# A one-core decode-and-prefill block on Trainium2: state chunks loaded early, masked B made up front, stores issued by ScalarE, first prompt tile turned inside the state stage

## The reference, cut to what matters

```python
proj = h @ w_in                       # z (2048 columns), xbc (3072), dt (32)
xbc = silu(causal_conv(xbc)); xs, Bm, Cm = split(xbc)
dt = softplus(dt + dt_bias); A = -exp(a_log)
# per head of 64 channels, chunks of 128 tokens, state of 64 x 128 per head:
A_cs   = cumsum(A * dt)
y_diag = (C . B) * exp(segsum) @ (xs * dt)
state' = state * exp(A_cs[last]) + B^T . (exp(A_cs[last] - A_cs) * xs * dt)
y_off  = exp(A_cs) * (C . state)
y = (y_diag + y_off + d_skip * xs) * silu(z), then group norm, @ w_out
```

## Time and profile before

| | before |
|---|---|
| median of 3 runs | 2064.46 us (2064.24 to 2065.48) |
| the profiled execution | 2061.77 us |
| its span, first to last instruction | 2060.1 us |
| PE busy | 1868.6 us, 91% |
| DVE busy | 1473.5 us, 72% |
| ACT busy | 1246.7 us, 61% |
| POOL busy | 177.9 us, 9% |
| mean granted clock of TensorE | 0.949 of full |

### The profile page before, as it was taken

One profiled execution on the slowest core, in us unless ns is written; L12 is line 12 of the kernel. 1 busy time (PEld: TensorE's weight loads), 2 busy tenths in 40 slices (PEclk: granted clock), 3 DMA queues, 4 the chain that ended last, 5 costly groups with the idle time before them and its releaser, 6 DMA issues.

```text
span 2060.1 us, 31992 instructions
## 1 busy us (share of the span) xinstructions
PE 1868.6 (91%) x10922; PEld 1608.2 (78%) x10922; DVE 1473.5 (72%) x1769; ACT 1246.7 (61%) x1604; POOL 177.9 (9%) x243
## 2 busy tenths in 40 slices
PE   6978889999889768789769999999999999999994
PEld 6968769999789548688558888888888888888883
DVE  7477436664478455753359888898988889888894
ACT  6555325443367124431268787888878787887873
POOL 2001101000124341010110000000000000000001
PEclk9989899999989889899889999999999999999997
DMA  7544667854434471156469999999999999999993
GB/s 276 193 133 159 243 255 283 352 166 141 160 98 155 170 262 59 46 190 236 184 230 386 370 380 372 380 356 374 378 360 380 374 385 354 372 376 357 393 366 144
DMA packets 151105, 558.74 MB, mean 271 GB/s; under 512 B 16496, under 2 KB 16496, under 8 KB 149568
## 3 DMA queue, kind: packets, MB, share of 16 engines
q1 hardware_dynamic: 139248, 508.58, 67.2%
q0 software_dynamic: 7200, 28.56, 3.7%
q10 hardware_dynamic: 4528, 20.05, 2.4%
HBM read 520.61 MB, written 36.52 MB: 270 GB/s over the span
## 4 chain that ended last, share of the span: by engine, by line
PE 77%; issue 8%; DVE 7%; DMA 4%; ACT 4%; POOL 1%; POOLq 0%; SPq 0%; ACTq 0%; DVEq 0%
PE ps L1663 23%; PE ps L1665 23%; PE ps L1664 23%; DMA raw<-in_stream 2%; DVE w_lo L1059 2%; ACT w_hi L670 2%; PE ps L1949 1%; PE ps L2064 1%; POOL rt L2108 1%; PE ps L1762 1%; PE ps L1793 1%; PE ps L1809 1%; PE ps L1694 1%; DMA y_rows<-ye 0%; PE ps L1784 0%
## 5 line engine op out<-in xcount | busy, mean ns | idle before, releaser
L1564 DVE TENSOR_TENSOR w_lo<-raw,w_hi 128x1024 fp32r<-128x1024 f32 x672 | 787.1, 1221 | 50.6 <-ACT w_hi L989 49.0
L989 ACT ACTIVATE w_hi<-raw 128x1024 fp32r<-128x1024 f32 x672 | 704.6, 1060 | 139.7 <-PE ps L1665 119.9
L1059 DVE TENSOR_TENSOR w_lo<-raw,w_hi 128x1024 fp32r<-128x1024 f32 x212 | 264.3, 1258 | 245.2 <-ACT w_hi L670 243.9
L1663 PE MATMUL ps<-w_hi,xe_hi 128*128 128x512 f32 x896 | 358.2, 400 | 4.7 <-DVE w_lo L1564 4.7
L1665 PE MATMUL ps<-w_hi,xe_lo 128*128 128x512 f32 x896 | 354.5, 396 | 0.0
L1664 PE MATMUL ps<-w_lo,xe_hi 128*128 128x512 f32 x896 | 354.0, 395 | 0.0
L670 ACT ACTIVATE w_hi<-raw 128x1024 fp32r<-128x1024 f32 x212 | 220.5, 1051 | 160.2 <-PE ps L1665 97.2
L1663 PE MATMUL ps<-h_hi,w_hi 128*128 128x288 f32 x928 | 286.1, 308 | 18.4 <-DVE h_lo L1085 14.1
L1664 PE MATMUL ps<-h_lo,w_hi 128*128 128x288 f32 x928 | 280.1, 302 | 0.0
L1665 PE MATMUL ps<-h_hi,w_lo 128*128 128x288 f32 x928 | 278.9, 301 | 0.0
L1663 PEld LDWEIGHTS ps<-h_hi,w_hi 128*128 128x128 f32 x928 | 180.1, 194 | 31.4 <-DVE h_lo L1085 16.8
(11 more groups left out here) (395 smaller groups left out, 2553.1 us busy)
## 6 DMA issues: line engine op xcount, KB each, us to landing
raw<-in_experts SPq DMA_DIRECT2D x672, 512.0 KB, 5.5
raw<-in_stream SPq DMA_DIRECT2D x264, 512.0 KB, 4.4
rest<-in_stream SPq DMA_DIRECT2D x28, 512.0 KB, 5.1
x_rows<-zeros ACTq DMA_DIRECT2D x1, 13824.0 KB, 57.7
out_ssd_s<-s_new POOLq DMA_DIRECT2D x16, 512.0 KB, 4.4
xs<-x_rows POOLq DMA_DIRECT2D x9, 512.0 KB, 4.8
y_rows<-ye POOLq DMA_DIRECT2D x9, 512.0 KB, 7.3
out_k<-kmem ACTq DMA_DIRECT2D x2, 1024.0 KB, 6.6
```

Of the source, the lines that this page charges most:

```text
L989: act.activation(w_hi[:, (NSPLIT + p) % HL, :], raw[:, slot, :], ACT.Copy) \
L1059: dve.tensor_tensor(w_lo[:, o % HL, :], landing_place(k), w_hi[:, o % HL, :].bitcast(F32), ALU.subtract).then_inc(lo_done, 1)
L1564: dve.tensor_tensor(w_lo[:, (NSPLIT + p) % HL, :], raw[:, (NRING + p) % RAW, :], w_hi[:, (NSPLIT + p) % HL, :].bitcast(F32), ALU.subtract) \
L1663: pe.matmul(out, l_hi, r_hi, start=start, stop=False)
```

## The change

- `GATES` becomes [4, 1, 1, 2, 2, 2, 1, 1, 2]: y off 0 and 1 come one z tile apart and earlier.
- The state chunks S0a, S0b and S1a leave the ring. They land in `soon`, 12 KB in the upper part of `zs` (the gates' buffer), and SyncE issues them ahead of xbc 10 once f2's last group is full. The ScalarE gates that write over them wait for y off and `sn_dec` of the chunk. `zs` tile 5 and later wait for S1a's users, tile 8 for S0b's, tile 12 for S0a's.
- AHEAD of the groups s state, y off and xt of tile 0 is capped at two past the need; the cap for the first state chunks starts three chunks later, and for later ones goes by the z tile instead of by the s state two before.
- Masked B of all eight sequences is made before the first add (`btm4` has eight places now). VectorE waits for the store of out_ssd_c there, over whose source `btm4` lies.
- GpSimd only makes the decayed states; ScalarE issues the two stores of batch b (`send`) after the z gates of b.
- acs and last are made once, for the samples and both prompt tiles together, last two xbc tiles after acs. All exps of dec and last_dec are made at the beginning of the state stage.
- xt of tile 0 (transposes and VectorE's products) moves to just before y off 7, into a buffer of its own; y off turn moves behind bt and cb of tile 0.

With the new plan AHEAD of s state 0 is z 6, of s state 1 z 7, 2 z 9, 3 z 11, 4 z 13, 5 z 14, 6 z 15; of the ScalarE gates z 4 and z 5 z 9, z 6 and z 7 z 10, z 8 and z 9 z 12, z 10 and z 11 z 13, z 12 z 15, z 13 ssd out's first chunk, z 14 and z 15 its fifth. In the ring, S1b follows xbc 23, S3a waits for S1b's slot, z 11 for S2a's, S5a for S3a's, S6b for S4a's, S7a for S5a's.

The diff, cut to its core:

```diff
-GATES = [4] + [2, 1] * (NB // 2)
+GATES = [4, 1, 1, 2, 2, 2, 1, 1, 2]
 assert sum(GATES) == KI
+
+SOON, SOON_AT = 3, 10
...
-    p += [(("acs", 2), "dve", 0), (("last", 2), "dve", 0), (("ab", 2), "dve", 0)]
-    p += [(("xbc", c), "act", 1) for c in range(SAMPLE_AT + 1, NXBC)]
+    p += [("acs", "dve", 0)]
+    p += [(("xbc", c), "act", 1) for c in range(SAMPLE_AT + 1, SAMPLE_AT + 3)]
+    p += [("last", "dve", 0), (("ab", 2), "dve", 0)]
+    p += [(("xbc", c), "act", 1) for c in range(SAMPLE_AT + 3, NXBC)]
...
     for b in range(NB):
         p += z[sum(GATES[:b + 1]):sum(GATES[:b + 2])]
+        if b == NB - 1:
+            p += [(("xt", 0, i), "dve", 0) for i in range(4)]
         p += [(("y off", b), "dve" if b == NB - 1 else None, 2)]
         p += [(("s state", b, g), "dve", 0) for g in range(GROUPS)]
-    p += [("y off turn", "dve", 0)]
     for t in range(2):
-        p += [(("acs", t), "dve", 0), (("last", t), "dve", 0)]
-        p += [(("xt", t, i), "dve", 0) for i in range(4)]
+        if t:
+            p += [(("xt", t, i), "dve", 0) for i in range(4)]
         p += [(("bt", t), "act", 0), (("cb", t), "dve", 0)]
+        if t == 0:
+            p += [("y off turn", "dve", 0)]
...
+    soon = [k for k in range(NSTAT) if PLAN[TAKER[k]][0][0] == "y off"][:SOON]
...
+        elif k in soon:
+            at.append(("soon", soon.index(k)))
...
+        xt = [at(f"xt{i}", [DI], F32, (S[2], S[0])[i]) for i in range(2)]
+        soon = at("soon", [SOON, CH], F32, S[6] + KI * NT * 4 - SOON * CH * 4)
...
-        btm4 = at("btm4", [2, P], F32, S[10] + 6144)
+        btm4 = at("btm4", [NB, P], F32, S[9] + 4096)
...
-            for i in range(2 * NB):
-                before = KEY["s state", i // 2 - 2, GROUPS - 1] if i >= 4 else KEY["s decay"]
+            for i in range(SOON, 2 * NB):
+                before = KEY["z", sum(GATES[:i // 2])] if i >= 4 else KEY["s decay"]
                 if before >= g:
                     cap = min(cap, ORDER[RING[PLACE[STATE_CHUNK[i]][1] + RAW]])
             key = PLAN[g][0]
+            if key[0] in ("s state", "y off") or key[:2] == ("xt", 0):
+                cap = min(cap, ORDER[NEED[g]] + 2)
...
+                if TAKER[i] == KEY["xbc", SOON_AT]:
+                    sp.wait_ge(full, KEY["f2", KD - 1] + 1)
+                    for k in STATE_CHUNK[:SOON]:
+                        sp.dma_start(landing_place(k), t["stream"][k, :, :]).then_inc(landing(k)[0], 16)
+                if kind == "soon":
+                    continue
...
                 for c in range(c0, c0 + n):
                     b = ready(("z", c), NT)
+                    for i in range(SOON):
+                        if 1152 * (c + 1) > 18432 - 4096 * (i + 1):
+                            act.wait_ge(full, KEY["y off", i // 2] + 1)
+                            act.wait_ge(sn_dec, i + 1)
                     act.activation(zs[:, c, :], b, ACT.Silu).then_inc(act_freed, 1)
...
             act.wait_ge(pre_done, 1)
+            act.activation(dec[:, :, :], dec[:, :, :], ACT.Exp).then_inc(dec_done, 1)
+            act.activation(cdec[:, :], last_dec[:, :], ACT.Exp).then_inc(dec_done, 1)
...
+            def send(b):
+                hi_upto(AHEAD[KEY["s state", b, GROUPS - 1]])
+                for half in range(2):
+                    k = 2 * (b % 2) + half
+                    act.wait_ge(sn_done, 4 * b + 2 * half + 2)
+                    act.dma_start(t["out_ssd_s"][b, half], s_new[k][:, :]).then_inc(state_out[k], 16)
+
             for b_ in range(NB):
                 gates(sum(GATES[:b_ + 1]), GATES[b_ + 1])
-            hi_upto(AHEAD[KEY["s state", NB - 1, GROUPS - 1]])
+                send(b_)
             for k in range(2):
                 act.wait_ge(state_out[k], 16 * (NB // 2))
...
+                sums = ready("acs", 3 * HEADS)
+                b = sums[:, 2 * HEADS:3 * HEADS]
                 quads = [slice(32 * g, 32 * g + 32) for g in range(GROUPS)]
+                dve.tensor_scalar(nacs[:, :, :].rearrange("p a h -> p (a h)"), sums[:, 0:2 * HEADS], -1.0, None, ALU.mult)
...
+                lasts = ready("last", 3 * HEADS)
+                b = lasts[:, 2 * HEADS:3 * HEADS]
+                dve.tensor_copy(last_dec[:, :], lasts[:, HEADS:2 * HEADS])
+                dve.tensor_tensor(dec[:, :, :].rearrange("p a h -> p (a h)"), lasts[:, 0:2 * HEADS],
+                                  acs[:, 0:2 * HEADS], ALU.subtract)
...
+            dve.wait_ge(out_done, 48)
             for bq in range(NB):
-                if bq >= 2:
-                    dve.wait_ge(full, KEY["s state", bq - 2, GROUPS - 1] + 1)
-                dve.tensor_scalar(btm4[:, bq % 2, :], bt4[:, :], par("in_seq")[:, bq:bq + 1], None,
+                dve.tensor_scalar(btm4[:, bq, :], bt4[:, :], par("in_seq")[:, bq:bq + 1], None,
                                   ALU.mult).then_inc(btm_done, 1)
+            for bq in range(NB):
                 if bq == NB - 1:
+                    token_major(0)
...
             dve.wait_ge(state_out[0], 16 * (NB // 2))
-            dve.wait_ge(out_done, 48)
 
             for tt, (c0, n) in enumerate(TOK[:2]):
-                b = ready(("acs", tt), HEADS, n)
                 if tt:
-                    dve.wait_ge(xd_done, tt)
...
+                out = open_group("acs", 3 * HEADS)
+                for tt in range(2):
+                    pe.matmul(out[:, tt * HEADS:(tt + 1) * HEADS], tri, adt[:, tt, :], start=True, stop=True)
...
+            def sample_decays():
+                quads = [slice(32 * g, 32 * g + 32) for g in range(GROUPS)]
+                out = open_group("last", 3 * HEADS)
+                pe.wait_ge(dve_freed, FREED[KEY["acs"]][1])
+                pe.matmul(out[:, 0:2 * HEADS], par("last"), acs[:, 0:2 * HEADS], start=True, stop=True)
...
+                if b == NB - 1:
+                    token_major(0)
...
-                    close(pe.matmul(out, btm4[qd, b % 2, :], xd4[qd, :], start=True, stop=True))
+                    close(pe.matmul(out, btm4[qd, b, :], xd4[qd, :], start=True, stop=True))
...
-            decayed(0)
             for b in range(NB):
-                if b + 1 < NB:
-                    decayed(b + 1)
-                for half in range(2):
-                    k = 2 * (b % 2) + half
-                    pool.wait_ge(sn_done, 4 * b + 2 * half + 2)
-                    pool.dma_start(t["out_ssd_s"][b, half], s_new[k][:, :]).then_inc(state_out[k], 16)
+                decayed(b)
             for tt, (_, n) in enumerate(TOK[:2]):
```

More of the change, by code:

```diff
@@ L586, in landing @@
             kind, n = PLACE[i]
-            if kind == "split":
-                return rest_landed[n], 16 * (1 + sum(PLACE[k] == PLACE[i] for k in range(i)))
-            return landed[n % RAW], 16 * (n // RAW + 1)
+            if kind == "ring":
+                return landed[n % RAW], 16 * (n // RAW + 1)
+            s = n if kind == "split" else RAW + n
+            same = (("split", s), ("soon", s - RAW))
+            return rest_landed[s], 16 * (1 + sum(PLACE[k] in same for k in range(i)))
         def landing_place(i):
             kind, n = PLACE[i]
+            if kind == "soon":
+                return soon[:, SOON - 1 - n, :]
             return rest[:, n, :] if kind == "split" else raw[:, n % RAW, :]
@@ L1348, in sample_sums @@
                     .then_inc(sdr_done, 1)
-                link(dve.tensor_copy(acs[0:32, :], b[0:32, :]))
+                link(dve.tensor_copy(acs[:, :], sums))
                 dve.engine_nop().then_inc(dve_freed, 1)
@@ L1352, in sample_sums @@
                     dve.tensor_copy(dt4[qd, :], dt[0:32, 2, 8 * g:8 * g + 8])
-                b = ready(("last", 2), HEADS)
+            def sample_decays():
[5 more added lines that the diff above has]
+                                  acs[:, 0:2 * HEADS], ALU.subtract)
                 for g, qd in enumerate(quads):
@@ L1412, in _ @@
                     dve.engine_nop().then_inc(dve_freed, 1)
[L1413 to L1416 removed]
             dve.wait_ge(state_out[0], 16 * (NB // 2))
[L1418 removed]
             for tt, (c0, n) in enumerate(TOK[:2]):
[L1421 removed]
                 if tt:
[L1423 to L1438 removed]
+                    token_major(1)
                 b = ready(("cb", tt), 4 * n, n)
@@ L1444, in _ @@
                 dve.engine_nop().then_inc(dve_freed, 1)
+                if tt == 0:
+                    b = ready("y off turn")
+                    ys = y[:, :, SEQ:NT].rearrange("p (g k) s -> p g k s", g=GROUPS)
+                    dve.tensor_tensor(ys, ys, b.rearrange("p (k g s) -> p g k s", g=GROUPS, k=4), ALU.add) \
+                        .then_inc(dve_freed, 1)
                 def mix(hb):
@@ L1866, in _ @@
                     sample_sums()
+                if c == SAMPLE_AT + 2:
+                    sample_decays()
             def gates(c0, n):
@@ L1869, in gates, with token_major @@
                     square(("z", c), h_hi, h_lo)
+            def token_major(tt):
+                c0, n = TOK[tt]
```

(15 more changed lines are left out.)

88 lines of the change are left out of this document (30 added, 58 removed).

## The result

| | before | after |
|---|---|---|
| median | 2064.35 us (2061.7 to 2065.48, 4 runs) | 2027.34 us (2025.39 to 2031.92, 4 runs) |
| profiled execution, span | 2061.77, 2060.1 us | 2029.11, 2027.4 us |
| mean granted clock | 0.949 | 0.955 |

The ratio is 0.983, interval 0.9819 to 0.9842: 37.0 us faster by the medians, 32.7 by the two profiled spans. Forecast were 41.3 and a time of 2023.0, range 2012 to 2041. The sign and, in the main, the mechanism held; the size was 4.3 us too good by the median.

What follows compares the result with a forecast made beforehand. The state stage was held by waits: VectorE's adds behind late weight chunks, TensorE behind masked B. Terms -6.1, -25.8, -8.2 and -1.2 sum to -41.3, from 2061.77 to 2020.5 us profiled, median 2023; range 2012 to 2041.

Steps and rivals of the forecast that it cites:

- Part A: Sums before the state stage: 10.4 instead of 16.5 us, -6.1; ends -3.8 (half clock comes anyway) and -6.7.
- Early loads: Three state chunks, 1.57 MB, loaded before the state stage: cost 0, seven ring slots then carry three chunks more.
- Part B: State stage: waits behind weight chunks, adds and masked B go, last s state ends about 745 instead of 770.8 us, -25.8.
- rival 3: State stage: early chunks do nothing because ring order binds as before; 2031 us, chance 0.06.
- transfer term: State stage: 35 transfers, 18.35 MB at 350 GB/s, take 52.4 us from the first store at 687, to 739.4.
- DMA ends last, not TensorE: State stage's end: DMA path, with landing and queue gaps, ends about 745 us, TensorE's summed work at 738.4.
- Masked B: State stage: all eight made up front beside z 3, removing the link from adds to masked B; TensorE waited 27.9 us.
- Rival 1: State stage: the s_new buffers' loop of adds, store and decay holds it; 2028 to 2037, say 2033 us, chance 0.23.
- Part C: First prompt tile: acs, a 4.26 us wait, last and xt's transposes leave TensorE's path, -8.2 us; ends -5 and -9.0.
- Part D: Second prompt tile: acs, gap and last go, -1.2 us; ends -0.8 and -1.5.
- lock rule: State stage: VectorE's low halves and GpSimd's decays lock shared ports, 1.65 us per low half; alone, the sum stands.
- rule on issuing engines: State stage: issuing on another engine saves only issuing time, so stores from ScalarE get no faster; 350 GB/s grants none.

Runs made afterwards that it cites:

- last_at_once: Changed kernel with last and ab directly behind acs again, still for all three tiles together; 2041.64 us.
- soon_off: Changed kernel with no early chunks, all 16 state chunks in the ring; 2027.56 us.
- gates_cap: Changed kernel with ScalarE and VectorE capped two chunks past the need before the gates of z 14, z 15 and the prompt's first groups; 2028.10 us.
- btm_in_turn: Changed kernel with masked B made batch by batch, just ahead of each batch's adds; 2025.40 us.
- link_alone: Kernel before the change plus only the cap of two chunks past the need before s state and y off; 2051.72 us, ratio 0.9948.
- pool_stores: Changed kernel with the stores of the new states issued by GpSimd again, behind the next batch's decays; 2041.49 us.
- spread_sums_send: spread plus the sums one xbc tile later and ScalarE's last two stores issued behind the prompt's first exp; 2012.95 us, ratio to before 0.976.
- spread: gates_cap with the cap kept through the first prompt tile and let go by one chunk per two heads; 2027.95 us.
- sums_later: Changed kernel with acs one xbc tile later, after xbc 8, and last and ab after xbc 10; 2022.36 us.
- far_ahead: Changed kernel without the cap of two chunks past the need before s state, y off and xt of tile 0; 2052.08 us.
- xt_late: Changed kernel with the first prompt tile's transposes and VectorE's products behind the last s state again; 2038.91 us.
- cap_sums_send: The counter-test: spread_sums_send with the cap of gates_cap in place of spread's; 2028.61 us.

## Why the prediction was right, and where it was not

By the profiled spans, 32.7 us measured for 41.3 forecast.

- **Part A**, forecast -6.1, measured 60.03 - 55.20 = -4.8. The waits went as forecast; the lower clock level through xbc 8 (window 602 to 604: 10 products in 2.00 us at 0.50) took 1.5 by the six other kernels with the same sums, in which the column is 53.67 to 53.69, a gain of 6.35. So -4.8 is inside the end of -3.8, and the half clock is not the rule. last_at_once confirms the term by its undoing, 6.9.
- **Early loads**, cost 0 and a small gain: the cost was right. The 7.5 us that part B counts for them (the distance to rival 3, chance 0.06) were too much: soon_off shows 0 to 4.
- **Part B**, forecast -25.8, measured -22.1. The span from y off 0 to the last s state was to be 62 and is 63.6. Another 1.9 were lost ahead of y off 0, where the samples' small products and the z tile behind them stood at 0.50 from 669.9 to 676.4 us (before only 676.4 to 679.5). The transfer term came out: 343 GB/s in the 55 us from 686 to 741 are 18.9 MB, where I had 18.35 in 52.4. "DMA ends last, not TensorE" is the step that was half right. The last landing did delay the last s state, by 5.0 us, and gates_cap shows what that was: chunks that nobody needed yet. TensorE took 53.2 us without the transposes, as summed, and 57.5 with them (gates_cap, 0.7 of it a visible wait), where 53.2 and 1.9 are 55.1. So the two limits lay closer than the rates suggested, and I had put the transposes' bank order at nothing.
- **Masked B** up front, listed as a link removed, is none by itself (btm_in_turn). The cap alone is a third of the gain (link_alone).
- **Rival 1**, the buffers' loop, is visible in the chain, and GpSimd waits 41.4 us for stores; it does not bound the stage at 63.6, as the stage is 6.1 us shorter in gates_cap with 34.8 us of the same waits.
- **Part C**, forecast -8.2, measured 13.19 - 5.22 = -8.0. **Part D** -1.2, measured 56.48 - 55.80 = -0.7, with all that lies in between.
- **The rest**: 2.5 us slower, forecast 0 within 3. 1.2 of them are in ssd out, which took 53.3 us at a mean clock of 0.94 against 52.1 at 0.97; the other 1.3 I did not trace.
- **The lock rule** of the Trainium skill ("SBUF — State Buffer", section "SBUF: two separate sides"), which spoke against the change, was outweighed as argued. The trace agrees with it: beside GpSimd's decays a low half of VectorE took 2.97 us at 662 us, and the 14 low halves from 650 to 745 us took 1.76 on average, where the 17 from 660 to 771 before took 1.35. Yet VectorE still stood idle for 18.7 us until TensorE had the adds' groups ready. **The rule on issuing engines** of the Trainium skill ("DMA: Bandwidth & Descriptors", section "Issuing engines are not separate DMA queues") held for the stage (pool_stores 64.33, after 63.60). It did not bear on the end: the issuer decides what GpSimd and ScalarE do next, and there it cost 5.2 us and the clock.
- **The signs**: no wait for masked B, xbc 8 reached ScalarE after 4.4 us idle instead of 10.8, and the last s state came 5.2 us ahead of the first exp, as forecast. The stage's DMA share is 0.88, just short of 0.9. The half clock through xbc 8, named as a sign that A is 3.8, did show in this profile.

The sum of misses: 1.3 + 3.7 + 0.2 + 0.5 + 2.5 = 8.2; the spans differ from the forecast by 8.6, of which 0.35 lies ahead of acs (599.9 for 599.6). The forecast's last sentence on its numbers, that half-clock stretches may shift by 3 us either way, had the right cause and too small a size. I looked for holes where before had them, and never asked what a hole in the prompt's first tile would cost. It costs 10 to 16 us by the prompt column (66.2 to 71.9 for 55.8). The change stands near that edge: its own tile ran at 1.00, while undoing any of three parts (stores, xt, last) brought the stretch in the profiled execution, and by times and clocks (0.948 to 0.952) in the others too. So most of their 12 to 14 us are not the part's own price. One execution each of soon_off and btm_in_turn, 12 us above its siblings, looks the same by its time.

## What to carry to other kernels

Read a stage's gain and the clock behind it apart: cut the span at fixed landmarks in both traces, because 6 us won in one stage can be hidden by 12 us of half clock in the next, as in gates_cap. An engine that splits weights ahead in program order holds up whatever stands behind it until the weights have landed. Here going six chunks ahead instead of two cost 12 to 25 us, and splitting four in a row instead of one per step made the hole that the counter-test priced. If executions of one kernel fall into two groups, compare their mean granted clocks, and look for a hole on TensorE, here of half a microsecond or more, at the head of a long dense stretch.

## What the runs showed of the hardware that I had not expected

- The lower clock level can outlast its cause by far. In gates_cap the holes of 2.09 and 3.16 us were followed by 27 us at 0.50, with TensorE busy for 0.98 of the time behind the second hole. All seven profiles with such a stretch have it last 20 to 31 us, and in each the clock rose while the eight 512-column products ran. Elsewhere, with 288-column products behind it, a stretch ended sooner once TensorE was busy throughout: in some 6 us (605.6 to 611.4 before, 669.9 to 676.4 after).
- Narrow products alone did not hold the clock down everywhere. In after and in link_alone it rose at the end of these two windows, in which TensorE was always busy, with products of 128 columns or fewer. Ahead of its window after had run the last s state's 512-column products, while link_alone had stood idle for 10.8 us:

```profile
744.30:748.30 4.00, 4.00 (x20) 4.00 (x21) 4.00 (x6) 1.88 (x3) 0.00 (x0) 0.50 0.83 285
763.50:767.60 4.10, 4.10 (x20) 4.10 (x21) 2.40 (x6) 1.51 (x2) 0.00 (x0) 0.51 1.03 421
```

So the width of the products is not shown to be what kept the prompt's tile at 0.50.
- The size of the hole that brings it is not sharp. At the first y products of the first prompt tile the profiled executions with no hole (before, link_alone, btm_in_turn) or one of 0.28 to 0.56 us (after, spread_sums_send, soon_off, spread) kept the clock, those with 0.98 (sums_later), 1.55 (last_at_once) and 2.09 to 5.20 us (the rest) lost it. (In far_ahead it fell at 760.7 us already, ahead of the hole of 2.43 and behind one of 2.78.) Holes of one length go either way: all 14 profiles have holes of 0.94 and 1.40 us at the end of the second prompt tile, and the clock fell there in four (link_alone, pool_stores, xt_late, cap_sums_send). By their times, three of five executions of sums_later kept the clock in the first tile, and five of six of spread lost it. What decides there is open.
- With stores and loads mixed, the engines moved 343 GB/s over 55 us, a little under the 350 that I had assumed and the 372 of the experts' pure loading. In gates_cap a window of 4 us has 425, at a share of 1.04.
